# Attention scores of a two-layer hybrid encoder: three float32r products of upper and lower parts, placed in the middle of a slot

## What is computed

```
q = apply_rope(rms_norm(q)) * 64 ** -0.5
k = apply_rope(rms_norm(k))
scores = einsum('bhcqd,bhckd->bhcqk', q_block, k)      # c: the two halves of a head
probs = softmax(scores)
weights = probs[:, :, 0] - lam * probs[:, :, 1]
o = weights @ v                                        # then a norm per head
```

## Time and profile before

| | us |
|---|---|
| median of three runs | 1439.61 |
| the profiled execution | 1438.98 |
| its span in the profile | 1437.2 |
| TensorE busy | 1404.3 |
| VectorE busy | 842.7 |
| GpSimd busy | 724.7 |
| ScalarE busy | 623.3 |

### The profile page before, as it was taken

One profiled execution on the slowest core, in us unless ns is written; L12 is line 12 of the kernel. 1 busy time (PEld: TensorE's weight loads), 2 busy tenths in 40 slices (PEclk: granted clock), 3 DMA queues, 4 the chain that ended last, 5 costly groups with the idle time before them and its releaser, 6 DMA issues.

```text
span 1437.2 us, 18656 instructions
## 1 busy us (share of the span) xinstructions
PE 1404.3 (98%) x6444; PEld 1119.2 (78%) x6444; DVE 842.7 (59%) x1051; ACT 623.3 (43%) x894; POOL 724.7 (50%) x551
## 2 busy tenths in 40 slices
PE   5999999999999999999999999999999999999999
PEld 4887777777788888888878877776777888888887
DVE  6666598555677667700267857973557677675001
ACT  6343455475444444422343335554744444443211
POOL 2597275426444444444577853752473444444443
PEclk9999999999999999999999999999999999999999
DMA  4212112113222222323222221121122223222323
GB/s 151 89 61 91 54 60 73 49 43 101 75 101 102 88 92 98 102 91 102 90 86 74 89 77 46 55 74 44 60 90 86 90 99 102 88 95 95 103 94 110
DMA packets 36820, 121.05 MB, mean 84 GB/s; under 512 B 4896, under 2 KB 5408, under 8 KB 36768
## 3 DMA queue, kind: packets, MB, share of 16 engines
q1 hardware_dynamic: 36480, 119.64, 24.9%
q10 hardware_dynamic: 288, 0.72, 0.1%
HBM read 114.05 MB, written 2.10 MB: 81 GB/s over the span
## 4 chain that ended last, share of the span: by engine, by line
PE 81%; POOL 5%; issue 5%; ACT 4%; DVE 4%; DMA 1%; SPq 0%; POOLq 0%; DVEq 0%; ACTq 0%
PE bank L494 23%; PE bank L496 22%; PE bank L495 22%; PE bank L578 3%; POOL wL L434 2%; PE bank L599 2%; PE bank L546 2%; PE bank L617 2%; PE bank L534 2%; POOL wL L428 1%; POOL rstd L358 1%; PE bank L587 1%; DVE QQ L1229 1%; PE bank L608 1%; ACT wH L758 1%
## 5 line engine op out<-in xcount | busy, mean ns | idle before, releaser
L434 POOL TENSOR_TENSOR wL<-raw,wH 128x1024 fp32r<-128x1024 f32 x142 | 342.3, 2411 | 420.4 <-ACT wH L766 357.9
L494 PE MATMUL bank<-hH,wH 128*128 128x512 f32 x1216 | 487.9, 401 | 25.2 <-POOL wL L428 12.1
L496 PE MATMUL bank<-hL,wH 128*128 128x512 f32 x1216 | 476.2, 392 | 0.0
L495 PE MATMUL bank<-hH,wL 128*128 128x512 f32 x1216 | 475.7, 391 | 0.0
L428 POOL TENSOR_TENSOR wL<-raw,wH 128x256 fp32r<-128x256 f32 x272 | 255.1, 967 | 188.7 <-ACT wH L758 188.7
L494 PEld LDWEIGHTS bank<-hH,wH 128*128 128x128 f32 x1216 | 229.5, 189 | 96.5 <-issue 39.4
L496 PEld LDWEIGHTS bank<-hL,wH 128*128 128x128 f32 x1216 | 229.5, 189 | 49.7
L495 PEld LDWEIGHTS bank<-hH,wL 128*128 128x128 f32 x1216 | 229.9, 189 | 44.8 <-issue 0.5
L766 ACT ACTIVATE wH<-raw 128x1024 fp32r<-128x1024 f32 x116 | 122.5, 1056 | 183.6 <-PE bank L496 180.9
L758 ACT ACTIVATE wH<-raw 128x1024 fp32r<-128x1024 f32 x95 | 100.4, 1057 | 150.7 <-PE bank L496 150.1
L494 PE MATMUL bank<-gH,wH 128*128 (+1 forms) x352 | 137.3, 390 | 0.1
(11 more groups left out here) (156 smaller groups left out, 1718.2 us busy)
## 6 DMA issues: line engine op xcount, KB each, us to landing
raw<-wts SPq DMA_DIRECT2D x211, 512.0 KB, 3.3
x<-xT SPq DMA_DIRECT2D x8, 256.0 KB, 5.4
swp<-K SPq DMA_DIRECT2D x32, 64.0 KB, 2.0
swp<-QO SPq DMA_DIRECT2D x32, 64.0 KB, 2.3
outT<-x SPq DMA_DIRECT2D x8, 256.0 KB, 2.0
raw<-wts ACTq DMA_DIRECT2D x1, 512.0 KB, 4.2
W<-pos SPq DMA_DIRECT2D x1, 256.0 KB, 7.4
R<-par SPq DMA_DIRECT2D x2, 109.0 KB, 3.6
```

What stands on the lines that cost most here:

```text
L434: pool.tensor_tensor(wL[:, s, :], raw[:, s, :], wH[:, s, :].bitcast(F32), ALU.subtract)\
L494: pe.matmul(out, wH[:, s, a:a + P], rhs_h, start=first, stop=False)
L495: pe.matmul(out, wL[:, s, a:a + P], rhs_h, start=False, stop=False)
L496: return pe.matmul(out, wH[:, s, a:a + P], rhs_l, start=False, stop=last)
```

## The change

Before the scores, query and key of each head are split into an upper part in float32r and a lower part, as is done with the weights. `part_high` is a ScalarE copy, first in the slot's list, two slots after the statistic (`PARTED`: slots 15, 16, 20, 21, 23, 24, 27, 28). `part_low` is a VectorE subtraction behind the eviction in the same slot, in place over the query or key. The upper parts lie over halves of KK and T that the recurrence has finished with; added waits guard these places (in `part_high`, in the eviction of the first gate unit, in `high_out`). The scores become three float32r products for each half of the head, with the halves alternating, and their place in the slot moves from before the token transposes to between the first half of the unit and the turn. They wait for `qk_low` instead of `scaled`.

```diff
--- before.py
+++ after.py
@@ -59,6 +59,8 @@
          23: ("hgo", 1), 24: ("dao", 0), 25: ("dk", 3), 26: ("dq", 3), 27: ("dao", 1), 30: ("dao", 2),
          31: ("hgo", 2), 32: ("hgo", 3), 34: ("dao", 3)}
 JOB = {job: j for j, job in enumerate(STATS.values())}
+PARTED = {s + 2: job for s, job in STATS.items() if job[0] in ("dk", "dq")}
+PART = {job: j for j, job in enumerate(PARTED.values())}
 OUT_HEADS = [("dao", 0), ("dao", 1), ("dao", 2), ("hgo", 0), ("hgo", 1), ("hgo", 2), ("hgo", 3), ("dao", 3)]
 FINISH = {31: (0, 1), 32: (2, 3), 33: (4, 5), 34: (6, 7)}
 LATE = 34
@@ -146,6 +148,7 @@
 def build(nc, xT, wts, cst, msk, par, lbl, pos, outT):
     ctx = ExitStack()
     mix = ExitStack()
+    parts = ExitStack()
     heads = ExitStack()
     ffn = ExitStack()
 
@@ -201,6 +204,13 @@
         ev = sb("ev", [P, S], F32, mix)
         W = sb("W", [P, S], F32, mix)
         mix.close()
+        KKr = sb("KKr", [P, 2, HEADS * S], F32R, parts)
+        sb("over_A_QQ", [P, 2 * TT * S + 2 * HEADS * S], F32, parts)
+        Tr = sb("Tr", [P, 2, HEADS * S], F32R, parts)
+        sb("over_HI_V", [P, 2 * TT * S], F32, parts)
+        QOr = sb("QOr", [P, HEADS, S], F32R, parts)
+        K2r = sb("K2r", [P, 2, S], F32R, parts)
+        parts.close()
         yH = sb("yH", [P, KT, S], F32R, heads)
         yL = sb("yL", [P, KT, S], F32R, heads)
         heads.close()
@@ -251,6 +261,8 @@
         a_msk = signal("a_msk", 28)
         av_mm = signal("av_mm", 4)
         oh_ready = signal("oh_ready", 4)
+        qk_high = signal("qk_high", 2 * HEADS)
+        qk_low = signal("qk_low", 2 * HEADS)
         sc_mm = signal("sc_mm", STEPS)
         neg_max = signal("neg_max", STEPS)
         exps = signal("exps", STEPS)
@@ -331,6 +343,19 @@
 
             return K2[:, hd % 2, :] if kind == "dk" else QO[:, hd, :]
 
+        def upper(kind, hd):
+
+
+
+            if hd % 2:
+                at = 0 if kind == "dk" else S
+                return KKr[:, 1, at:at + S]
+            return Tr[:, 0 if kind == "dk" else 1, 0:S]
+
+        def lower(kind, hd):
+
+            return K2r[:, hd % 2, :] if kind == "dk" else QOr[:, hd, :]
+
         def out_head(kind, hd):
 
             return head(QQ, 0, hd) if kind == "hgo" else QO[:, hd, :]
@@ -591,13 +616,16 @@
                     def scores(a):
                         hd, qt = divmod(a, 4)
                         if qt == 0:
-                            pe.wait_ge(*scaled.at(l, JOB[("dq", hd)] + 1))
+                            pe.wait_ge(*qk_low.at(l, PART[("dq", hd)] + 1))
                         if a:
                             pe.wait_ge(*exps.at(l, a))
-                        for c in range(2):
-                            r = slice(HD * c, HD * c + HD)
-                            m = pe.matmul(bank[4 + c][:], QO[r, hd, qt * P:qt * P + P], K2[r, hd % 2, :],
-                                          start=True, stop=True)
+                        qH, kH = upper("dq", hd), upper("dk", hd)
+                        qL, kL = lower("dq", hd), lower("dk", hd)
+                        at = slice(qt * P, qt * P + P)
+                        for n, (q, k) in enumerate(((qH, kH), (qL, kH), (qH, kL))):
+                            for c in range(2):
+                                r = slice(HD * c, HD * c + HD)
+                                m = pe.matmul(bank[4 + c][:], q[r, at], k[r, :], start=n == 0, stop=n == 2)
                         m.then_inc(sc_mm.sem, 1)
 
                     def turn(a):
@@ -673,14 +701,14 @@
                     for s in range(SLOTS):
                         if item_of(s) is not None:
                             item(item_of(s))
-                        if step_of(s) is not None:
-                            scores(step_of(s))
                         if tokens_of(s) is not None:
                             to_tokens(tokens_of(s))
                         half = unit_half if s < N_IN else out_half
                         half(s, 0)
                         if s == LATE:
                             stat(STATS[s])
+                        if step_of(s) is not None:
+                            scores(step_of(s))
                         if step_of(s - 1) is not None:
                             turn(step_of(s - 1))
                         half(s, 1)
@@ -866,6 +894,19 @@
                             act.activation(kx[:].rearrange("p r t -> p (r t)").rearrange("p (n two h) -> p n two h", two=2, h=h),
                                            crossing(KK, 2 * pair, 0, h, 0, 2 * TT), ACT.Copy).then_inc(kx_ready.sem, 1)
 
+                    def part_high(job):
+
+                        kind, hd = job
+                        act.wait_ge(*scaled.at(l, JOB[job] + 1))
+                        if hd == 0:
+                            act.wait_ge(*hg_q.at(l, 4))
+                            act.wait_ge(*hg_k.at(l, 2))
+                        elif hd == 1:
+                            act.wait_ge(*lv_mm.at(l, 22))
+                        else:
+                            act.wait_ge(*sc_mm.at(l, 4 * (hd - 1)))
+                        act.activation(upper(kind, hd), rope_tile(kind, hd), ACT.Copy).then_inc(qk_high.sem, 1)
+
                     def back(a):
                         use = BANK6[("turn", a)]
                         act.wait_ge(*bank6_full.at(l, use + 1))
@@ -893,6 +934,8 @@
                         kind, hd = OUT_HEADS[p]
                         if p == 0:
                             act.wait_ge(*lv_mm.at(l, 44))
+                        if p == KT // 2:
+                            act.wait_ge(*sc_mm.at(l, STEPS))
                         act.wait_ge(*(gated.at(l, hd + 1) if kind == "hgo" else scaled.at(l, JOB[(kind, hd)] + 1)))
                         act.activation(yH[:, p, :], out_head(kind, hd), ACT.Copy).then_inc(yH_ready.sem, 1)
 
@@ -916,6 +959,8 @@
                         for k in range(4):
                             square(l, 0, k)
                     for s in range(SLOTS):
+                        if s in PARTED:
+                            part_high(PARTED[s])
                         if s:
                             high_now(s + 1)
                         if s == 1:
@@ -1114,6 +1159,7 @@
                         elif kind == "hg":
                             dst = gs(hd)
                             if hd == 0:
+                                dve.wait_ge(*sc_mm.at(l, 12))
                                 dve.wait_ge(*hg_q.at(l, 10))
                                 dve.wait_ge(*hg_k.at(l, 8))
                         else:
@@ -1143,6 +1189,13 @@
                         dve.wait_ge(*rstd_ready.at(l, j + 1))
                         dve.tensor_tensor(q, q, rstd[:, j % 2, :], ALU.mult).then_inc(scaled.sem, 1)
 
+                    def part_low(job):
+
+                        kind, hd = job
+                        q = rope_tile(kind, hd)
+                        dve.wait_ge(*qk_high.at(l, PART[job] + 1))
+                        dve.tensor_tensor(lower(kind, hd), q, upper(kind, hd).bitcast(F32), ALU.subtract).then_inc(qk_low.sem, 1)
+
                     def norm(job):
 
 
@@ -1258,6 +1311,8 @@
                     for s in range(N_IN + 4):
                         if 0 < s <= N_IN:
                             evict(s - 1)
+                        if s in PARTED:
+                            part_low(PARTED[s])
                         if l == 0 and s == 3:
                             bounds()
                         if s == 4:
```

## The result

The changed kernel takes 1453.63 us (median of four runs, 1453.06 to 1455.2) against 1439.47 (1438.82 to 1440.43): ratio 1.0101, 95% interval 1.0089 to 1.0113. It is 1% slower, and the forecast of 1456 lies 2.4 us above it. The profiled execution took 1453.4, with a span of 1451.6.

A forecast was written before the change was run, and what follows sets the result against it. TensorE, busy 98% of the span, was taken as the bound: 1438.98 us - 5.4 for cheaper products + 22.4 of waits (11.2 a layer) = 1456.0. Own range 1447 to 1469 (64%); 80% range 1443 to 1472.

The forecast's parts named there:

- slot 15: Head 0's key: token transposes wait on `part_high` ahead of the bank read, 1.7 us a layer.
- slot 20: Head 1's key: chain of 7.8 us against 6.94 and a longer item, wait 0 to 0.9, taken 0.
- slot 21: Head 1's query: scores wait 0.7 to 1.1 us for `part_low`, the turn 0.7 more for `combine`; taken 1.8.
- slot 23: Head 2's key: chain from late scores to bank read 9.05 us against TensorE's 6.94; transposes wait 2.1.
- slot 33: ScalarE is full; its bank read comes 0.6 us later and savings of slots 31 and 32 are lost: 0.8.
- The products: Six float32r products replace two float32 ones; pairing on 64 rows gives 0.89 us a step, 0.17 less; 32 steps, -5.4.
- The chain and where it decides: Scores 2.9 us later delay maxima, growth, rotary, `part_high` and bank read; transposes wait once the chain exceeds 6.94 us.
- slots 24, 27 and 28: The same chain makes the transposes wait 1.5, 1.5 and 1.8 us a layer, range 1.0 to 3.0 each.
- Hidden: Rival: the chain from scores to bank read is hidden, only the products count: -5.4 us, 1434; 8%.
- Half the waits: Rival: waits half of 22.4 us as late engines catch up, 1445; 15% together with near no change.
- Serial halves: Rival: 64-row float32r products do not pair, 0.69 us a step above 0.89, 1478; 13%.
- Long rotary: Rival: VectorE's rotary stays 4.14 us in five slots a layer, 11.6 more, 1468; within forecast's own range, no separate chance.

The follow-up runs named there:

- three combinations: Changed kernel with growth first and upper parts behind `fin`, 1447.43 us; with scores at start except step 4, copies behind `fin`, 1443.31; same, head 1's query copied first, 1442.89.
- the last one: Changed kernel with head 0's parts in slot 16, only head 2's query behind `fin`, all scores at the slot's start: 1435.95 us.
- slot 15 by itself: Changed kernel with only the copy of head 0's key, in slot 15, moved behind `fin`: 1453.42 us.
- the last two: Changed kernel with head 0's parts in slot 16, only head 2's query behind `fin`, scores at slot's start: except step 4, 1434.2 us; all, 1435.95.

## Why the prediction was right, point by point

| a layer, us | predicted | measured |
|---|---|---|
| slot 15 | 1.7 | 1.66 |
| slot 20 | 0 | 0.16 |
| slot 21 | 1.8 | 2.3 |
| slot 23 | 2.1 | 1.8 |
| slot 24 | 1.5 | 1.1 |
| slot 27 | 1.5 | 1.3 |
| slot 28 | 1.8 | 1.2 |
| slot 33 | 0.8 | 1.25 |
| waits, sum | 11.2 | 10.8 |
| saved by 16 steps | 2.7 | 3.5 |

A measured wait is the slot's distance after, less that of before, plus the 0.22 that a slot saves; slot 15's is the stretch from its item to its transposes, 4.18 against 2.52.

- *The products.* 0.89 a step was forecast and 0.89 stands in the timeline. The kernel with the scores at the start shows the saving of 0.17 alone. With the move it is 0.22: the missed 0.05 is the move's own, and the kernel with the move alone has it too. The likely reason, argued only: the scores' 64-row products are then neighbours of the turn rather than of the item.
- *The chain and where it decides.* The mechanism was right: moved scores, late rotary, `part_high` ahead of `fin`, bank 6, transposes. Both halves of it were shown, by taking the copy away from ahead of `fin` (13.5 us of waits gone) and by taking the move away (slots 23, 27 and 28 at 10.99 or less). The sizes in slots 24, 27 and 28 were 0.2 to 0.6 too large. In slot 23 the growth took 1.89 (206.76 to 208.65) where 2.38 was in the sum (it took 2.46 in the earlier trace rows); GpSimd had ended its own growth at 204.91 and its split at 208.18, so the rotary behind it was the short one, as the sum had it: 2.98 was taken and it was 2.89 (208.65 to 211.54).
- *Slot 21.* The term that was mis-sized downward most: `combine`, put at 1.6. TensorE's, VectorE's and GpSimd's timelines of the changed kernel there:

```profile
191.75 0.50 PE L628 MATMUL bank<-KKr 64*128 64x512 f32 x2
...
194.97 0.63 PE L636 MATMUL bank<-C,W 128*128 128x128 f32 x4 [2.25 <-DVE W L1308]
```

```profile
190.09 0.89 DVE L1197 TENSOR_TENSOR QOr<-QO,KKr 128x512 fp32r<-128x512 f32 x1
190.90 0.15 DVE L1303 RECIPROCAL sm<-sm 128x2 f32<-128x2 f32 x1
191.09 1.07 DVE L1304 TENSOR_TENSOR sm<-sm,lamc 128x1 f32<-128x1 f32 x1
192.20 1.48 DVE L1305 TENSOR_SCALAR E<-E,sm 128x512 f32<-128x512 f32 x1
193.72 1.10 DVE L1308 SCALAR_TENSOR_TENSOR W<-E,sm 128x512 f32<-128x512 f32 x1
```
```profile
189.16 1.27 POOL L480 TENSOR_TENSOR T<-T 128x256 f32<-128x256 f32 x2 [4.56 <-PE bank L603]
190.39 3.01 POOL L486 TENSOR_TENSOR KK<-KK,T 128x512 f32<-128x512 f32 x2
193.36 3.44 POOL L453 TENSOR_TENSOR wL<-raw,wH 128x256 fp32r<-128x256 f32 x4
```

  It took 3.85 (190.90 until the next operation at 194.75), all of it beside GpSimd, whose growth stands at 189.16 to 193.4, with its split behind it: the scaling of one value per row takes 1.07, and L1305, 0.49 without GpSimd (at 199.44 in the kernel with the growth first), 1.48. The queue ahead of it was over-sized: the scores waited for nothing in mid-slot (191.75), where 0.7 to 1.1 was in the sum. So 2.25 for the turn in place of 0.7 + 1.1. The Trainium skill (SBUF — State Buffer, Who interferes with whom) says that VectorE with two SBUF inputs contends with a GpSimd instruction that reads SBUF, and that one may block for the whole of the other. The 1.07 for a 128x1 operation agrees, to the hundredth: the GpSimd instruction that ran when it started ended 1.06 behind that start (last section). By it one should ask of every VectorE operation that is moved, not of the rotary alone, what GpSimd does at its new time; I asked it for the rotary.
- *Slot 33* cost 1.25, not 0.8: the turn waits 1.4 for ScalarE's read where it waited 0.67, and the savings of the steps before it are lost in that. It is the move's alone, as the kernel with the move alone has the same 1.4.
- *Slot 20* was nearly hidden, 0.16 within its 0 to 0.9.
- *The sum.* With the terms in their measured sizes it is 1438.98 - 7.0 + 21.6 = 1453.6, where the profiled execution took 1453.4. The 2.4 us between that and the forecast are 1.6 of larger savings and 0.8 of shorter waits. That 1453.6 and 1453.4 agree so closely is in part luck: the slots' distances give 13.5 for both layers, 1.1 less than these terms, and the later start of 0.9, which no term has, fills most of that. It is luck too that TensorE's clock, which the prediction did not weigh, makes no difference: one stretch gone (at 1097), one come (at 843), but one or two more in six of the experiments (last section).
- *The rivals.* Hidden (1434): refuted, it decides under 6.94 and the chain was above it in four slots. Half the waits (1445): refuted, they came to 96% of the 22.4 that was summed. Serial halves (1478): refuted by both orders. Long rotary (1468): refuted in the changed kernel, 2.89; in the kernel with the growth first it is 3.66, so the long one exists and its condition was the right one.

The weak part of the account is the other direction. Of the eleven expectations, the misses (the upper part behind `fin`, growth first, three combinations, slot 15) are all of one kind: a removed wait was counted as gained in full. It came back in part, as the same work then met GpSimd, the eviction, or VectorE's queue a slot later; and all of them but the last had one or two stretches of low clock more, up to 1.7 us each.

## What to carry to other kernels

With queues in a fixed order, a step that is moved and a copy that is added can each be nearly free, 1.8 and -0.3 us here, and cost 14.0 together, if one makes an operation late and the other puts that operation ahead of a shared bank's release. Cost the pair by the chain from the moved step to the release against what the waiting engine still has to do. And where a new operation can stand before or behind the release, look at who waits for its own result: here it was first in the list for seven of eight copies and behind the release for head 2's query (slot 24 is 11.20 with its copy first in the kernel with the parts alone, 10.99 with it behind `fin` in the last one), and head 0's key was best copied a slot later.

## What the runs showed of the hardware

- *The clock after a wait.* The changed kernel's stretches around 843 us, in the same columns as above:

```profile
843.00:846.00 3.00, 3.00 (x9) 2.32 (x8) 2.96 (x3) 1.33 (x5) 3.00 (x4) 0.50 0.00 0
846.00:850.00 4.00, 4.00 (x19) 3.35 (x18) 2.39 (x4) 0.89 (x2) 0.88 (x1) 0.97 0.38 135
```

  After slot 15's wait TensorE is granted 1.2 GHz for 3.4 us, though busy throughout, and 9 matmuls start in 3 us where 19 start in the 4 behind them. Each such stretch cost 1.4 to 1.7 us. In layer 1 the same wait of 2.24 has none behind it. Nor is the length of the wait what decides: TensorE waits 1.94 for the lower part of a unit in the kernel before (until 388.37) and in the one with the scores at the start but one (until 390.96), and the stretches behind it are:

```profile
389.40:393.00 3.60, 3.60 (x17) 3.00 (x16) 1.75 (x4) 2.37 (x3) 1.63 (x1) 1.00 0.42 146
```
```profile
392.00:395.50 3.50, 3.50 (x10) 2.73 (x9) 1.73 (x4) 2.28 (x3) 1.55 (x1) 0.51 0.42 147
```

  the first of the kernel before, at full clock, the second of the other, at half. Between start-up and the span's end the thirteen profiled kernels have 48 waits of TensorE of 1.9 to 2.4 us and 23 such stretches. Each stretch begins at the end of one of these waits (from 0.5 before it to 1.4 behind); the other 25 waits have none. The kernels before and after have one stretch each, as have those with the parts alone, the halves in turn, slot 15 by itself and the last two; two have the move alone and growth first; three have the upper part behind `fin`, the growth with it, and the two with the scores at the start but one. Which of the waits are followed by one, these runs leave open; a saving of less than 2 us a layer can be lost in it.
- *64-row products in float32r* of 512 columns take 0.23 to 0.24 a pair in either order, about half of the 0.43 of a float32 pass.
- *A one-column VectorE operation* (the 128x1 product of `combine`, two inputs in SBUF) took 0.16 alone and 1.07 beside GpSimd. It took as long as GpSimd's running instruction still had, and 0.02 more: 1.07 with 1.06 left (191.09 in the changed kernel), 0.88 with 0.86 left (258.45), 0.38 with 0.36 left (189.72 with the growth first), 0.59 with 0.57 left (195.40 in the kernel before). At 164.03 in the changed kernel, where it had started 0.13 before GpSimd's, it took 0.16.
